# Float32r passes on high and low parts for the RWKV and dilated projections, split by ScalarE and GpSimd

## The reference, cut to what matters

```python
def second_block(x, mem, ...):
    n = rmsnorm(h, norm_mix_g[l])
    proj = (n @ w_in[l]).astype(f32)
    ...                                                        # a shift by one token on the RWKV columns
    (p_r, p_k, p_v, p_wd, p_ad, p_gd, q, k, v, gate_r, gate_a) = jnp.split(proj, bounds, axis=-1)
    y_rwkv = rwkv7_mix(p_r, p_k, p_v, p_wd, p_ad, p_gd, ...)   # a scan over tokens, 16 heads of 64
    y_attn = dilated_mixture(hd(q), hd(k), hd(v))              # three groups, softmax over all
    merged = (jax.nn.sigmoid(gate_r) * (y_rwkv @ p_rwkv[l].astype(f32))
              + jax.nn.sigmoid(gate_a) * (y_attn @ p_attn[l].astype(f32)))
    h = h + (merged @ w_out[l].astype(f32)).astype(h.dtype)
    ...                                                        # memory cross attention, feed-forward
```

## Time and profile before

| | |
|---|---|
| median of 3 runs | 2769.64 us (2767.25 to 2769.79) |
| profiled execution: own time / span of the core | 2770.47 / 2768.7 us |
| mean granted TensorE clock | 0.991 |
| busy: PE, PEld, DVE, ACT, POOL | 2689.2, 1945.4, 1662.4, 656.2, 202.4 us |
| the seven passes with `ahead` (1403.8 to 1836.6 us) | 432.8 us, 61.8 each |
| last pass / dilated attention / first part of the merge | to 1890 / to 2029.7 / from 2029.7 us |

### The profile page before, as it was taken

How to read it: one execution, slowest core, us unless ns; L and a number is a source line. 1 busy time by engine, 2 the same in 40 slices (tenths; PEclk the granted TensorE clock), 3 DMA queues, 4 the chain that set the end, 5 groups by cost and what they waited for, 6 DMA issues and landing times.

```text
span 2768.7 us, 43450 instructions
## 1 busy us (share of the span) xinstructions
PE 2689.2 (97%) x17783; PEld 1945.4 (70%) x17783; DVE 1662.4 (60%) x2208; ACT 656.2 (24%) x1147; POOL 202.4 (7%) x219
## 2 busy tenths in 40 slices
PE   7999899999999999999999999999989999999998
PEld 4545556888878878888655555574667888788887
DVE  4888766565466565554466666654465665655554
ACT  4234433111010121110233323322341211211102
POOL 2000321000000000000011111110000000100001
PEclk9999999999999999999999999999999999999999
DMA  7675203333323323333211111112123333233332
GB/s 263 196 249 188 77 24 102 95 93 100 97 82 99 97 85 91 98 95 97 78 42 42 35 35 35 35 58 73 37 59 97 93 112 102 69 99 99 98 92 76
DMA packets 394394, 255.54 MB, mean 92 GB/s; under 512 B 19767, under 2 KB 376720, under 8 KB 394128
## 3 DMA queue, kind: packets, MB, share of 16 engines
q1 hardware_dynamic: 391456, 246.78, 29.8%
q0 software_dynamic: 2320, 5.11, 0.6%
q10 hardware_dynamic: 480, 1.64, 0.2%
HBM read 250.61 MB, written 2.10 MB: 91 GB/s over the span
## 4 chain that ended last, share of the span: by engine, by line
PE 88%; DVE 7%; issue 2%; ACT 2%; DMA 1%; SPq 0%; DVEq 0%; ACTq 0%
PE PS L846 15%; PE PS L847 15%; PE PS L848 15%; PE PS L1675 5%; PE PS L1650 3%; PE PS L861 3%; PE PS L863 3%; PE PS L862 3%; DVE ARENA L2638 2%; PE PS L833 2%; PE PS L1764 1%; PE PS L1656 1%; PE PS L1358 1%; PE PS L1882 1%; PE PS L1538 1%
## 5 line engine op out<-in xcount | busy, mean ns | idle before, releaser
L872 DVE CAST WH<-W 128x1024 fp32r<-128x1024 f32 x304 | 213.3, 702 | 402.8 <-PE PS L848 359.1
L874 DVE TENSOR_TENSOR WL<-W,WH 128x1024 fp32r<-128x1024 f32 x304 | 374.6, 1232 | 10.4
L847 PE MATMUL PS<-XNL,WH 128*128 128x512 f32 x960 | 373.6, 389 | 0.0
L846 PE MATMUL PS<-HH,WH 128*128 128x512 f32 x672 | 262.0, 390 | 0.2 <-DVE HL L3023 0.2
L848 PE MATMUL PS<-HH,WL 128*128 128x512 f32 x672 | 261.5, 389 | 0.0
L847 PE MATMUL PS<-HL,WH 128*128 128x512 f32 x672 | 261.4, 389 | 0.0
L847 PEld LDWEIGHTS PS<-XNL,WH 128*128 128x128 f32 x960 | 180.2, 188 | 37.7 <-issue 0.7
L846 PE MATMUL PS<-XNH,WH 128*128 128x512 f32 x512 | 199.2, 389 | 0.0
L848 PE MATMUL PS<-XNH,WL 128*128 128x512 f32 x512 | 199.2, 389 | 0.0
L846 PE MATMUL PS<-XN2H,WH 128*128 128x512 f32 x448 | 176.9, 395 | 7.5 <-issue 7.5
L848 PE MATMUL PS<-XN2H,WL 128*128 128x512 f32 x448 | 174.5, 389 | 0.0
(11 more groups left out here) (520 smaller groups left out, 4640.3 us busy)
## 6 DMA issues: line engine op xcount, KB each, us to landing
ARENA<-in_ada_w SPq DMA_DIRECT2D x80, 512.0 KB, 5.2
W<-in_ffn_w SPq DMA_DIRECT2D x64, 512.0 KB, 3.8
W<-in_w_in SPq DMA_DIRECT2D x51, 512.0 KB, 4.5
W<-in_ffn_w_gate SPq DMA_DIRECT2D x44, 512.0 KB, 3.6
W<-in_ffn_w_up SPq DMA_DIRECT2D x44, 512.0 KB, 3.6
W<-in_ffn_w_down SPq DMA_DIRECT2D x32, 512.0 KB, 3.8
W<-in_sc_w_in SPq DMA_DIRECT2D x24, 512.0 KB, 3.7
ARENA<-in_ada_w SPq DMA_DIRECT2D x8, 1024.0 KB, 19.5
```

The source lines that it names most:

```text
L846: nc.tensor.matmul(dst, WH[:, h, c], hi(k), start=(start and k == 0), stop=False)
L847: nc.tensor.matmul(dst, WH[:, h, c], lo(k), start=False, stop=False)
L872: nc.vector.tensor_copy(WH[:, h, :], W[:, s, 0:D]).then_inc(parted, 1)
L874: nc.vector.tensor_tensor(WL[:, h, :], W[:, s, 0:D], WH[:, h, :], ALU.subtract).then_inc(freed[s], 1)
```

## The change

All 42 units become three float32r passes (`split_fill`) over weights that two other engines split. ACT copies the fp32 weights, rounded, to a high part (`weight_high`, L2459: one 128x1024 copy, or two of 128x512). POOL subtracts that from the weights and leaves the low part in the slot itself (`weight_low`, L1153: likewise one subtraction or two). PE waits for POOL where it waited for the DMA. The high and low parts of `XN` (`XNH` by ACT, `XNL` by DVE, eight instructions each) are made in the front, just behind each `n`; before, they were made for the merge, at the end of stage 4.

The space for the parts has to come from somewhere: `YR` now lies in `X`'s place, and POOL's queue stores x to DRAM (`x_kept`, 2 MB) ahead of stage 2 and loads it back in the merge, where POOL scales all eight tiles in a row; the eight L1126 are gone from the passes. The weights of the dilated units ahead of stage 4 have one buffer (`TAIL`) where they had two. The dilated value units are now feature-major like the rest, each with four PE transposes (`value_turns`) and one more ACT copy. The squares of x move ahead of the norm's root on ACT. One DVE reciprocal moves from the front to a step of stage 4. The merge multiplies by its gates first, then by `p_rwkv` and `p_attn`.

```diff
+            def weight_high(slot, buf, p_act, step):
+                for own, high_part, _ in weight_parts(slot, buf):
+                    ins = nc.scalar.activation(high_part, own, ACT.Copy)
+                ins.then_inc(p_act.sem, p_act.step(step))
...
+            def weight_low(slot, buf, p_act, high, p_pool, step, at=0):
+                pool.wait_ge(p_act.sem, p_act.done(high, at))
+                for own, high_part, low_part_ in weight_parts(slot, buf):
+                    ins = nc.gpsimd.tensor_tensor(low_part_, own, high_part, ALU.subtract)
+                ins.then_inc(p_pool.sem, p_pool.step(step))
...
+            def split_fill(slot, buf, ks, dst):
+                low = low_weights(slot)
+                for k in ks:
+                    h, c = k // 4, slice(k % 4 * P, (k % 4 + 1) * P)
+                    high = high_weights(buf, h)
+                    nc.tensor.matmul(dst, high[:, c], XNH[:, k, :], start=(k == 0), stop=False)
+                    nc.tensor.matmul(dst, high[:, c], XNL[:, k, :], start=False, stop=False)
+                    mm = nc.tensor.matmul(dst, low[:, h, c], XNH[:, k, :], start=False, stop=(k == KD - 1))
+                return mm
...
             for u in range(3):
-                pe.wait_ge(landed[ring.slot("rw_first", u)], ring.arrived("rw_first", u))
-                unit_product(pe, "rw_first", u, 0, bank[u], xn, KD, ...)
+                pe.wait_ge(rf_pool.sem, rf_pool.done(step))
+                for k in range(KD):
+                    if u == 0:
+                        pe.wait_ge(norm_mix2.dve.sem, norm_mix2.dve.done(f"l{k}"))
+                    mm = split_fill(s, buf, (k,), bank[u])
...
 # POOL, the passes
             for i in range(RW_PAIRS - 1):
+                weight_low(ring.slot("rw", 1), "B", rw_act, "hk", rw_pool, "lk", i)
+                weight_low(ring.slot("rw", 2), "A", rw_act, "hv", rw_pool, "lv", i)
                 level_masks(i, i, rw_pe, rw_dve, rw_pool)
-                scaled(i)
+                weight_low(None, "B", rw_act, "hd", rw_pool, "ld", i)
+                weight_low(ring.slot("rw", 0), "A", rw_act, "hr", rw_pool, "lr", i)
...
 # PE, a pass
-                    early = lambda ks: projection(2, ks, "raw1")
-                    late = lambda ks: dilated(i, ks, "gg")
+                    early = lambda ks: projection(2, ks, "raw1", "A", "lv")
+                    late = lambda ks: dilated(i, ks, "gg", "B", "ld")
                 else:
-                    early = lambda ks: dilated(8, ks, "dila")
-                    late = lambda ks: second_first(ks)
+                    early = lambda ks: dilated(7, ks, "dila", "B", "l7")
+                    late = lambda ks: dilated(8, ks, "gg", "A", "l8")
...
 # PE, the merge
+            operands = ((xn_hi, xn_lo, KD, {}), (xn_hi, xn_lo, KD, {}),
+                        (lambda k: YRH[:, k, :], lambda k: YRL[:, k, :], KD, {0: "y3", 4: "y7"}),
+                        (lambda k: YAH[:, k, :], lambda k: YAL[:, k, :], 2, {0: "a1"}))
```

More of the change, by code:

```diff
@@ L1670, in projection @@
+                def projection(u, ks, read, buf, low):
                     s = ring.slot("rw", u)
                     if ks[0] == 0:
-                        bank_read(read)
-                        pe.wait_ge(landed[s], ring.arrived("rw", u, i))
-                    for k in ks:
-                        mm = nc.tensor.matmul(bank[7], tiles(s)[:, k, :], xn(k), start=(k == 0), stop=(k == KD - 1))
+                        if u:
+                            pe.wait_ge(p_act.sem, p_act.done(read, at))
+                            pe.wait_ge(p_pool.sem, p_pool.done(low, at))
+                        else:
+                            pe.wait_ge(rw_act.sem, rw_act.before("dil", i))
+                            if i:
+                                pe.wait_ge(rw_pool.sem, rw_pool.done("lr", i - 1))
+                            else:
+                                pe.wait_ge(rf_pool.sem, rf_pool.done("l1"))
+                    mm = split_fill(s, buf, ks, bank[7])
@@ L1708, in pair_pass, with dilated @@
-                if ahead:
-                    projection(0, range(KD), "before")
-                else:
-                    dilated(7, range(KD), "before")
+                def dilated(u, ks, read, buf, low):
+                    if ks[0] == 0:
+                        pe.wait_ge(p_act.sem, p_act.done(read, at))
+                        pe.wait_ge(p_pool.sem, p_pool.done(low, at))
+                    mm = split_fill(None, buf, ks, bank[7])
+                    if ks[-1] == KD - 1:
+                        mm.then_inc(dw_used, 1)
@@ L1713, in pair_pass @@
+                if ahead:
+                    projection(0, range(KD), "dil", "A", "lr")
+                else:
+                    s = ring.slot("dil", 0)
+                    pe.wait_ge(rz_act.sem, rz_act.done("e6"))
+                    pe.wait_ge(rw_pool.sem, rw_pool.done("lr", RW_PAIRS - 2))
+                    split_fill(s, "A", range(KD), bank[7]).then_inc(freed[s], 1)
                 if i == 0:
@@ L1753, in pair_pass @@
                 if ahead:
-                    projection(1, range(0, 5), "raw0")
+                    projection(1, range(0, 5), "raw0", "B", "lk")
                 for l in levels:
@@ L1826, in pair_pass @@
                 mm.then_inc(p_pe.sem, p_pe.step("rq"))
+                if not ahead:
+                    pe.wait_ge(p_act.sem, p_act.done("e7", at))
+                    gate_products()
                 def inside_rows(tiles_of):
@@ L1865, in pair_pass @@
                 nc.tensor.matmul(bank[1], PAIR_ONES, CSQ, start=True, stop=True).then_inc(p_pe.sem, p_pe.step("var"))
+                if i == 6:
+                    pe.wait_ge(p_act.sem, p_act.done("dil", at))
+                    value_turns(DIL0, 6).then_inc(rz_pe.sem, rz_pe.step("t6"))
+                elif not ahead:
+                    pe.wait_ge(p_act.sem, p_act.done("late", at))
+                    value_turns(DIL0, 8).then_inc(p_pe.sem, p_pe.step("t8"))
             for i in range(RW_PAIRS - 1):
@@ L3183, in pair_pass @@
                 dve.wait_ge(p_dve.sem, p_dve.done("yb", at))
+                dve.wait_ge(kept, 16)
+                if not ahead:
+                    dve.wait_ge(dl_act.sem, dl_act.done("u0"))
                 y = YR[:, i, :] if isinstance(i, int) else YR[:, ds(i, 1), :].rearrange("p a t -> p (a t)")
```

353 lines of the change are left out of this document (229 added, 124 removed).

## The result

The changed kernel takes 2778.65 us (median of 8 runs, 2774.11 to 2786.19) against 2770.24 for the kernel before (8 runs beside it, 2767.25 to 2773.12): ratio 1.0029, 95% interval 1.0019 to 1.0039. A second set on another chip gave 2784.39 (4 runs) against 2769.92 (13 runs), 1.0053 (1.0037 to 1.0070). So it is slower by 0.3 to 0.5%, some 8 to 14 us. Predicted were 2772 us, with a chance of 0.34 for slower by more than 5.5 us, which is what came.

A forecast was written before the change was run, and what follows sets the result against it. In the passes DVE's chain, not busy-looking PE, was taken to set p00; PE bound the dilated attention. Terms +8.5 + 2 + 0.3 + 4.2 − 11.1 − 1.5 = +2.4, say +2 on 2770.47, gave 2772 us, range 2748 to 2790.

The forecast's parts named there:

- a period above 63: Sign of error in the passes: a longer period means more clock loss, or `lk`, `ld`, `lr` on the path.
- The clock behind the gap: In each pass, PE's idle gap of about 4 us brings one half-rate spell, +1.65 us; bounds 0 and +3.4.
- rival 3: Passes: the clock falls for two spells each, +1.7 × 7 = +12 us on top, 2784 us; chance 0.24.
- Rival 2: Passes: DVE is locked but the clock stays full; total −9 to −10 us, 2761 us; chance 0.2.
- Six passes: Six full passes: −2.9 fills, +1.55 later p00, +1.65 clock, +0.3 us a pass; +2 in all.
- The front: Before the first pass: POOL and DVE alternate, first product at about 1376.8, p00 8.5 us later; bounds +3 and +11.
- Entering the last pass: Seventh pass into the last: `e6` and `l7` delay the masks, +3.3 us; fills save 3.0; net +0.3.
- e6: Entering the last pass: one more copy ahead of ACT's exponentials, which delays them by 1.8 us.
- The last pass: First late product waits for `h8` and `l8`, 4.4 us; transposes +0.5, clock +1.8, fills −1.4 −1.1: +4.2.
- The dilated attention: PE is the bound here: units 1 to 5 save 7.2 us, value units 6 to 8 save 3.9; −11.1.
- The merge: Gates first removes 2.36 us idle; DRAM load and POOL scalings beside DVE cost about +1; net −1.5 us.
- rival 1: Passes: DVE's chain is not held up, a pass saves 3.6 us; −31 in all, 2739 us; chance 0.12.

The follow-up runs named there:

- lv_late: Changed kernel with POOL's `lv` in the passes moved behind the first level's masks, waiting for DVE's last mask product: 2757.43 us, 0.9952 of the kernel before.
- lv_quarters: Changed kernel with `lv` of the passes made by four 128x256 POOL subtractions instead of one 128x1024, same place: 2766.99 us, 0.9985 of the kernel before.
- gap_fill: Changed kernel with unit 1's first five k run twice in each of seven passes, once for nothing: 2771.69 us, 1.0009 of the kernel before.
- last_pass: Changed kernel with ACT's high part `h8` ahead of the gate copy `gg` in the last pass: 2775.97 us, 1.0022 of the kernel before.
- merge_wait: Changed kernel with PE waiting for ACT's sigmoids, not DVE's products, ahead of the merge's gate products: 2773.14 us, 1.0022 of the kernel before.
- rw_fp32: Changed kernel with the RWKV units of seven passes as single fp32 matmuls again, on x's high part alone: 2767.02 us, 0.9991 of the kernel before.

## Why the prediction was right, and where it was off

- **DVE's chain sets p00, and `lv` holds it.** Shown three ways: the instruction's 2.65 us, lv_late (0.69, 12 us less over the passes' gaps) and lv_quarters. The port rule of the Trainium skill, page SBUF — State Buffer, section "SBUF: two separate sides", that I had weighed agrees: the loser waits for one instruction's end, 0.99 beside a quarter and 2.65 beside the whole.
- **`lr` was put at nothing.** "`lk`, `ld` and `lr` meet only DVE instructions that read PSUM or have slack, and cost nothing": `lr` meets L3229 or L3231, which read SBUF and lead to the mean. It holds one of them in each pass, by 2.2 us in the second and by 0.6 to 1.2 in the four after it, and the 2.2 are most of what makes the second pass 63.8 us long. The prediction's own sign for this, a period above 63, came in that pass. No run moved `lr` alone, so its share in the other passes is not shown.
- **The clock behind the gap.** Taken as one spell a pass, 1.65. gap_fill measured 1.5 on one spell. All five passes of the first trace have one, and two passes of the second trace have two, as rival 3 had it; as a whole that trace is 3.1 us longer than the first, as much as two spells more are worth. Rival 2 (full clock) is out for a gap of 3.5; it holds for lv_late's 1.55.
- **Six passes** came to +3.2 against +2. The second pass alone is 1.4 us above the next longest, most of it by `lr`.
- **The front** (+6.6 against +8.5): the mechanism was right, the size 2 too much; the first product came at 1375.1 and not 1376.8, which is most of it.
- **Entering the last pass** (+3.2 against +0.3). The +3.3 of `e6` and `l7` came as forecast: the seventh pass's mean to p00 takes 22.2 us, before 18.9. In the trace it stands as 1.4 (mean to transposes, 10.4 against 9.0 in the passes) and as L3292's 2.12. What was mis-sized is the credit of 3.0 for the fills: p00 to the mean takes 42.3 us, before 42.4. The seventh pass has two spells at half clock of its own (0.66 from 1792.3 to 1802.3), which my sum charged to six passes alone; in gap_fill, with none, the same stretch takes 39.9.
- **The last pass** (+4.2 as predicted). My wait and spell were 4.4 + 1.8 = 6.2. last_pass took 6.4 us out between p00 and the mean by one move on ACT, 3.45 of it wait, so the clock was worth 2.9 and not 1.8, and the wait less than 4.4. The rest, −2.0 in my sum, is −2.3 by the same run against the kernel before.
- **The dilated attention** (−11.4 against −11.1) is the one stage where PE was the bound, and the only one where the conversion paid what a count of passes promised. With the stage's code unchanged it takes 126.1 to 130.2 us in the other traces, so an agreement to 0.3 is partly luck.
- **The merge** is the step that failed most: "Net −1.5" was +3.6. I had left the 0.73 us between iterations as they were. With the gates first, the short product (p_attn, 1.36 us) comes last, and PE's wait for DVE's product, which had always been covered, became visible: 0.63 more, seven times, 4.4 us. merge_wait shows it: without that wait the gaps are 0.69. The scalings make the first gap 1.7 longer still, where I had about 1; that they are its cause I judge from their place and from the stretched splits beside them, as no run moved them.
- **Luck.** The stated range is 42 us wide, so it says little that the time fell inside. The sum was +2.4 and came out at +8.2 for the profiled executions: the merge, the entry to the last pass and the passes were 9.2 too low together, and the front, the dilated attention and the rest 3.4 too high. The rest's −1.2 goes with one spell at half clock that the kernel before has there (0.83 from 2262 to 2272) and the changed one has not. In the sum of rival 1, moreover, the last pass stands at −1 without a reason, where my own term is +4.2.

What decides between one spell and two is not the gap's length: in the second trace PE waits 3.5 us ahead of p00 in the third to the sixth pass, and two of them have two spells, two have one. What does decide is not shown. None followed in the passes of lv_late, with gaps of 1.0 to 1.55 us; one each followed gaps of 2.0 to 2.3 in lv_quarters.

## What to carry to other kernels

When PE looks 97% busy, ask at each wait what else would end there: here slow matmuls only filled the time of a DVE chain, and a faster fill bought idle time and then a lower clock. Work given to POOL cost DVE here up to the length of POOL's longest instruction wherever DVE read two SBUF operands. DVE instructions that read one operand from PSUM were not held (L3301 takes 0.69 us beside a POOL instruction, 0.68 alone), so place POOL's work beside those, or cut it small. Check this for every instruction that is added, not only for the one that looks worst. When units are reordered, look at which product is now the last and short one, and give each wait the true last reader of its buffer.

## What the runs showed that I had not expected

A DVE tensor_scalar with one SBUF operand (L3235) was held as well. It takes 0.49 us alone (in the front of rw_fp32), 0.71 in the passes, where it lies beside POOL's masks, and took 2.46 beside a POOL subtraction of 128x1024 in the front. A reciprocal, which also reads one SBUF operand (L3342), was not: 3.35 us beside POOL and alone. And an idle stretch of PE costs more than itself by an amount that differs between executions: of two traces of the same kernel, one has one pass of five above 63 us, the other three, and two of these three have a second spell at half clock.
